# Three output-projection tiles of sparse attention are issued inside its last three slots, and two bank rings change roles

## The reference, cut to what matters

```
def nsa_layer(h, g_norm, w_in, w_out, ...):
    q, gate, bgate = jnp.split(rmsnorm_2(h, g_norm) @ w_in, ...)
    o = gates[..., 0:1] * o_c + gates[..., 1:2] * o_s + gates[..., 2:3] * o_w   # 16 heads x 128
    y = (silu(gate) * o) @ w_out                                                # 2048 -> 1024
    return h + y

def per_layer_embedding(h, p_i, g, w_gate, w_emb):
    gate = jax.nn.sigmoid(rmsnorm_2(h, g) @ w_gate)
    return h + gate * (p_i @ w_emb)
```

## Time and profile before

| | |
|---|---|
| median of 3 runs | 1336.76 us (1335.0 to 1338.62) |
| the profiled execution's own time | 1335.06 us |
| its span, first to last instruction | 1333.3 us |
| PE busy | 1252.2 us, 94% of the span |
| DVE busy | 893.3 us, 67% |
| ACT busy | 642.2 us, 48% |
| mean granted TensorE clock | 0.976 |

### The profile page before, as it was taken

How to read it: one execution, slowest core, us unless ns; L and a number is a source line. 1 busy time by engine, 2 the same in 40 slices (tenths; PEclk the granted TensorE clock), 3 DMA queues, 4 the chain that set the end, 5 groups by cost and what they waited for, 6 DMA issues and landing times.

```text
span 1333.3 us, 19422 instructions
## 1 busy us (share of the span) xinstructions
PE 1252.2 (94%) x8046; PEld 1118.0 (84%) x8046; DVE 893.3 (67%) x1361; ACT 642.2 (48%) x999; POOL 11.6 (1%) x27
## 2 busy tenths in 40 slices
PE   4988899999999999999999999899899999998897
PEld 4976798999888769899989977678798989997685
DVE  4986568877756556887779656635585646666454
ACT  5464655555544334555555333335534545555343
POOL 0000000000000000000000000000000000000000
PEclk9988899999989999999999999989998999999999
DMA  8420244655443223465545545335264722222241
GB/s 348 159 95 1 104 154 157 219 189 190 163 153 127 86 86 132 150 216 187 189 175 182 179 167 173 126 126 187 98 222 158 260 96 96 95 96 95 95 160 61
DMA packets 28135, 198.44 MB, mean 149 GB/s; under 512 B 3216, under 2 KB 3344, under 8 KB 4752
## 3 DMA queue, kind: packets, MB, share of 16 engines
q1 hardware_dynamic: 28048, 197.21, 41.5%
HBM read 196.14 MB, written 1.05 MB: 148 GB/s over the span
## 4 chain that ended last, share of the span: by engine, by line
PE 78%; DVE 10%; ACT 5%; issue 5%; DMA 1%; DVEq 0%; SPq 0%; POOL 0%; POOLq 0%; ACTq 0%
PE bank L678 22%; PE bank L679 21%; PE bank L680 21%; DVE WL L1502 3%; ACT WH L1151 3%; PE bank L943 2%; PE bank L1125 1%; DMA RAW<-wstream 1%; DVE work L1688 1%; PE bank L1105 1%; PE bank L882 1%; PE bank L1096 1%; PE bank L1027 1%; PE bank L1123 1%; PE bank L893 1%
## 5 line engine op out<-in xcount | busy, mean ns | idle before, releaser
L1502 DVE TENSOR_TENSOR WL<-RAW,WH 128x2048 fp32r<-128x2048 f32 x181 | 414.2, 2290 | 217.7 <-ACT WH L1151 217.3
L1151 ACT ACTIVATE WH<-RAW 128x2048 fp32r<-128x2048 f32 x181 | 345.6, 1911 | 236.2 <-PE bank L680 223.3
L678 PE MATMUL bank<-XH,WH 128*128 128x256 f32 x1264 | 362.0, 286 | 12.1 <-DVE XL L1538 7.4
L679 PE MATMUL bank<-XL,WH 128*128 128x256 f32 x1264 | 358.8, 284 | 0.0
L680 PE MATMUL bank<-XH,WL 128*128 128x256 f32 x1264 | 358.7, 284 | 0.0
L678 PEld LDWEIGHTS bank<-XH,WH 128*128 128x128 f32 x1264 | 243.6, 193 | 16.8 <-DVE XL L1538 8.0
L679 PEld LDWEIGHTS bank<-XL,WH 128*128 128x128 f32 x1264 | 243.7, 193 | 0.5
L680 PEld LDWEIGHTS bank<-XH,WL 128*128 128x128 f32 x1264 | 243.6, 193 | 0.0
L678 PE MATMUL bank<-WH,MH 128*128 128x512 f32 (+1 forms) x544 | 202.9, 373 | 11.0 <-DVEq L1621 7.4
L679 PE MATMUL bank<-WL,MH 128*128 128x512 f32 (+1 forms) x544 | 200.3, 368 | 0.0
L680 PE MATMUL bank<-WH,ML 128*128 128x512 f32 (+1 forms) x544 | 199.7, 367 | 0.0
(11 more groups left out here) (254 smaller groups left out, 1566.3 us busy)
## 6 DMA issues: line engine op xcount, KB each, us to landing
RAW<-wstream SPq DMA_DIRECT2D x181, 1024.0 KB, 4.8
con<-consts SPq DMA_DIRECT2D x1, 1681.0 KB, 17.8
x<-x_in SPq DMA_DIRECT2D x1, 1024.0 KB, 4.9
work<-mem_in SPq DMA_DIRECT2D x1, 1024.0 KB, 14.2
out_dram<-xn SPq DMA_DIRECT2D x2, 512.0 KB, 2.7
par<-params SPq DMA_DIRECT2D x1, 868.0 KB, 6.2
gfree<-g_final SPq DMA_DIRECT2D x1, 512.0 KB, 18.7
xn<-p_in SPq DMA_DIRECT2D x2, 256.0 KB, 3.9
```

Source lines behind the costliest of these rows:

```text
L678: mm(o, ah, bh, start=start, stop=False)
L679: mm(o, ah, bl, start=False, stop=False)
L1151: act_fn(WH[:, t % RING, :], RAW[:, t % RING, :], ACT.Copy).then_inc(w_rounded, 1)
L1502: tt(WL[:, t % RING, :], RAW[:, t % RING, :], WH[:, t % RING, :].bitcast(F32), ALU.subtract).then_inc(w_split, 1)
```

## The change

The first three output-projection tiles move from behind the loop into slots 14, 15 and 16, between the transposes and `On`. For that the four accumulators `no` are taken in slot 14, out of ring A, and the transposes of slots 14 to 16 are taken out of ring B. ACT and DVE round and split the next tiles inside slots 15 to 17 instead of behind the loop. The wait for `lo_done` moves to the seventh tile. In `ple`, for both layers, the four `pe` uses are taken two by two around `turn`, with semaphores of their own.

```diff
@@ plan_banks
         if 0 <= s - 1 < NSA_H:
-            aux("A", ("Ts", s - 1), "dve")
-            aux("A", ("Tw", s - 1), "act")
+            ring = "A" if s < NSA_H - 2 else "B"
+            aux(ring, ("Ts", s - 1), "dve")
+            aux(ring, ("Tw", s - 1), "act")
+        if s == NSA_H - 2:
+            acc("no", ("no", 7), "A")
...
-    acc("no", ("no", 7))
     finish("no", 9)
...
 def ple(u, turn, acc, finish, l, n):
-    for q in range(4):
-        u.append(("A", ("pe", l, q), "dve", ("pe", l)))
+    for q in (0, 2):
+        u.append(("A", ("pe", l, q), "dve_values", ("pe", l)))
     turn(n, 1)
+    for q in (1, 3):
+        u.append(("A", ("pe", l, q), "dve_turn", ("pe", l)))
@@ PE, ple
-                o = [take(("pe", l, q)) for q in range(4)]
+                o = {q: take(("pe", l, q)) for q in (0, 2)}
                 pe.wait_ge(*lo_a.next())
                 gemm_d_half(("pe", l), 0, o, PH, PL, 0, True, True)
                 turn(n, 1)
+                o |= {q: take(("pe", l, q)) for q in (1, 3)}
                 gemm_d_half(("pe", l), 1, o, PH, PL, 0, True, True)
@@ PE, slots
                 if s // 2 + 1 < 8:
                     gemm_t((("nq", "ng")[s % 2], s // 2 + 1), XH, XL)
+                else:
+                    c = s - (NSA_H - 2)
+                    if c == 0:
+                        o_out = [take(("no", q)) for q in range(4)]
+                    gemm_d(("no", c), o_out, MH, ML, 2 * c, c == 0)
...
-            o = [take(("no", i)) for i in range(4)]
-            pe.wait_ge(*lo_a.next())
-            for c in range(7):
-                gemm_d(("no", c), o, MH, ML, 2 * c, c == 0)
-            gemm_d_last(("no", 7), o, MH, ML, 14, None, 9)
+            for c in range(3, 7):
+                if c == 6:
+                    pe.wait_ge(*lo_a.next())
+                gemm_d(("no", c), o_out, MH, ML, 2 * c, False)
+            gemm_d_last(("no", 7), o_out, MH, ML, 14, None, 9)
@@ ACT, end of slot s
                 if s and (s + 1) // 2 < 8:
                     upto((("ng", "nq")[s % 2], (s + 1) // 2))
-            for c in range(7):
+                elif s >= NSA_H - 1:
+                    upto(("no", s - NSA_H + 1))
+            for c in range(3, 7):
                 upto(("no", c))
@@ DVE, end of slot s
                 if s and (s + 1) // 2 < 8:
                     upto((("ng", "nq")[s % 2], (s + 1) // 2))
+                elif s >= NSA_H - 1:
+                    upto(("no", s - NSA_H + 1))
             sync()
             low_signal()
-            for c in range(6):
+            for c in range(3, 6):
                 upto(("no", c))
```

## The result

The changed kernel takes 1318.34 us (median of 4 runs, 1317.94 to 1321.49) against 1336.19 (4 runs, 1335.0 to 1338.62): a ratio of 0.9869, 95% interval 0.9848 to 0.9890, 17.9 us by the medians. The profiled execution took 1318.41 us, its span 1316.6, which is 16.7 less than before; the sum was 15.2.

The account below looks back on a forecast made before the run. TensorE, busy 94% of the span, bounds the kernel; its idle and low-clock time is the gain. Three tiles off the tail (16.32 us) less a 1.11 us later start give 15.2 us: 1336.76 to 1321.6 us, range 1319.4 to 1326.0.

Parts of the forecast that it names:

- The tile's price: Output-projection tile of 24 matmuls on TensorE: 5.44 us without a break, 5.61 as a filler inside a slot.
- the edges: Gaps on both sides of projection matmuls inside a slot: 0.17 us for each filler.
- the timeline: TensorE's new starts from slot 14 on: tail at 1251.66, 1.11 us later, but three tiles (16.32 us) shorter.
- What must be ready: Copies for `On` ready with 1.3 us to spare; splits of tiles 2 and 4 just in time, margins about 0.2 us.
- Banks and `ple`: Ring B's banks freed 0.9 us or more ahead, ring A's also in time, embedding uses reordered: cost 0.
- `lo_done`: Drain signal at 1256.9, its wait moved ahead of tile 6 at 1268.0: the 1.72 us wait goes.
- Slowness: Groups behind TensorE's idle waits in slots 14 to 16 run at the lower clock: 1.81 + 0.79 + 1.47 = 4.07 us.
- How the numbers follow: Whole-kernel time: median 1336.76 less 15.2 gives 1321.6 us; profiled execution 1335.06 would become 1319.9.
- B: Weights come late at filler 2 and tile 4: up to 4.2 us lost, 1325.8 us; chance 0.06.
- C: Ring B makes TensorE wait at the transposes, two slots losing 2.7 us each: 1327.0 us; chance 0.04.
- D: Lower clock stays through the 26.7 us filler stretch: slower, 1340.8 to 1348 us; chance 0.03.
- E: No net gain: the saving is given back in the embedding or at the end; chance 0.02.

Follow-up runs that it names:

- the late weights: Changed kernel with its three fillers kept, but ACT and DVE round and split the tiles one slot later: 1334.24 us, ratio 0.9988 to the kernel before.
- rings alone: Changed kernel's ring swap and embedding order, but all eight output-projection tiles behind the loop: ratio 0.9998 to the kernel before, stretch 338.89 us.
- the kernel with dummies: Kernel before plus 16 matmuls that nothing reads in each of slots 14 and 15, ahead of the value products: 1330.6 us, ratio 0.9967.

## Why the prediction fell short

- **The tile's price, the edges, the timeline:** right. 15.21 us in the profiled stretch against 15.2, each start within 0.15 us of the list once the earlier shift is taken off.
- **What must be ready:** right. No wait in the stretch; the two ties came out 0.2 us ahead, and the late weights show what they guard.
- **Banks and `ple`:** right at 0 (rings alone 0.9998). **`lo_done`:** right; at tile 3 it would have waited 5.18 us.
- **Slowness, 4.07 us in the sum seen from the other side:** mis-sized as a term of the median, though right for its trace. It is that of one execution. In two of four profiles of the kernel before the stretch with the same waits took 2.8 us more, 2.6 of them in the groups of slot 16, and the kernel with dummies, which removes this term for slots 14 and 15 and hardly anything else, gains 4.4 or 7.2 us. The sum took the trace's blocks as they stood, up to the start of the tail at 1250.55, so it inherited the cheaper case.
- **How the numbers follow:** the step that failed. The 15.2 us of the profiled execution (1335.06, hence 1319.9) were subtracted from 1336.76, a median of three runs and 1.7 us higher. That base was too high: the same kernel later had medians of 1334.47 (23 runs), 1334.97 (13) and 1334.91 (11), while the changed one stayed (1318.34, then 1318.57). 15.2 off these gives 1319.3 to 1319.8, so 1.8 to 2.3 us of the 3.2 by which the forecast missed are the base, more than the 1.7 that the range gave the median. The last 0.9 to 1.4 us are less than the second price (2.8) and within what the measurement leaves open (a ratio of 0.9848 to 0.9890 is 14.7 to 20.3 us), so their cause is not shown. The forecast also took what lifts other executions for untouched by the change, and part of it is the same slowness, which the change removes. The range had at its low end only the filler's 0.5 us and 1.7 for the median; it had no room for the stretch's second price (2.8) or the first part's chance (178.6 to 181.1 over the profiles with these instructions). 1318.4 of the profiled execution is 1335.06 - 15.2 - 1.5, the last term being the first part's.
- **Rivals:** B, C, D and E did not happen. For E, from the norm behind the output projection to the last one it is 27.97 us (1282.25 to 1310.22) and was 27.94, so nothing is given back there. The prediction cites the Trainium skill ("TensorE: Matmul & The Clock Gate") twice, and this trace bears out neither passage. Section A second HAM failure mode: psum-queue depth-cycling tells of a bf16 kernel whose clock swung; here the granted clock stayed at 1.00 in the stretch. Section Back-to-back issue gap has about 131 ns a matmul, by which the estimate was 3.1 us a tile; a filler took 5.66 us.

How often the kernel before pays the dearer price stays open: two of four profiles (and the cheaper price in the one with the rings alone) are too few. By the medians the change gave 17.9 us in the first comparison and 15.9 in the second (23 runs of before), between the two savings of 15.2 and 18.0.

## What to carry to other kernels

Where TensorE idles in a trace, look at how the work behind the idle stretch differs from the same work elsewhere: that is a second price, and it varies from execution to execution, so sum it as a range and put that range on the side of the gain. Take the time that the saving is subtracted from out of more than three runs: here three gave 1336.76 and 23 gave 1334.47, which was most of the miss. Independent matmuls in such a stretch take both prices away, but only as far as the slot would have idled, and only if the preparation of their weights moves with them: one slot late here cost 14.9 of 15.2 us. The gain was shown on this one kernel and one core.

## What the runs showed of the hardware that had not been expected

- Between the same waits, alike within 0.01 us each, the same small groups took either 339.1 or 341.9 us of stretch, two profiles each, by whether the granted clock was up again in slot 16 (0.91 twice, or 0.77 and 0.74, from 1240 to 1260).
- Sixteen matmuls that nothing reads, twice, made the kernel before 4.3 us faster by the medians, though its waits ended no sooner.
- A wait of 5.18 us in front of dense 512-column matmuls cost 7.8 us, one pair of 10.0 us cost 14.9: about half as much again as the wait itself. Behind the first, the matmuls started 0.43 us apart for 4.3 us (1256.90 to 1261.16), then 0.23.
